# Shared expert of a mixture-of-experts step: three products of high and low parts instead of one float32 product, and a ring of four for its sums

## What is computed

```python
def swiglu(x, wg, wu, wd):
    return (jax.nn.silu(x @ wg) * (x @ wu)) @ wd

routed = routed_experts(hf, eidx, gw, w_e_gate, w_e_up, w_e_down, blk)
shared = swiglu(hf, w_s_gate, w_s_up, w_s_down)
return (routed + shared).astype(h.dtype).reshape(B, S, D)
```

## Time and profile before

| | us |
|---|---|
| median of 3 runs (2080.31 to 2085.21) | 2081.19 |
| the profiled execution | 2073.48 |
| its span, first to last instruction | 2071.7 |
| PE busy | 1910.6 |
| DVE busy | 1318.2 |
| ACT busy | 996.6 |

### The profile page before, as it was taken

How to read it: one execution, slowest core, us unless ns; L and a number is a source line. 1 busy time by engine, 2 the same in 40 slices (tenths; PEclk the granted TensorE clock), 3 DMA queues, 4 the chain that set the end, 5 groups by cost and what they waited for, 6 DMA issues and landing times. The chain is left out here.

```text
span 2071.7 us, 38132 instructions
## 1 busy us (share of the span) xinstructions
PE 1910.6 (92%) x13128; PEld 1493.1 (72%) x13128; DVE 1318.2 (64%) x1974; ACT 996.6 (48%) x1537; POOL 759.1 (37%) x672
## 2 busy tenths in 40 slices
PE   7999899969799999999898989998999999999994
PEld 5787778857455689888687637777777777777773
DVE  4389767775789831111557636776777777777772
ACT  6322123356576621111334116766777766776762
POOL 2111123343445211100026713455436645445642
PEclk9999999989899999999999999999999999999997
DMA  7488831066577859870633258999999999999995
GB/s 238 139 287 268 275 121 42 19 189 182 188 225 230 265 194 291 270 249 21 216 107 103 85 212 297 352 350 319 350 356 356 349 341 354 348 353 343 345 324 141
DMA packets 170943, 501.87 MB, mean 242 GB/s; under 512 B 26326, under 2 KB 71956, under 8 KB 144396
## 3 DMA queue, kind: packets, MB, share of 16 engines
q1 hardware_dynamic: 128164, 353.65, 47.2%
q0 software_dynamic: 31680, 80.82, 15.5%
q10 hardware_dynamic: 10992, 66.02, 9.5%
HBM read 437.87 MB, written 120.75 MB: 270 GB/s over the span
## 5 line engine op out<-in xcount | busy, mean ns | idle before, releaser
L2769 DVE TENSOR_TENSOR w_gu_lo<-turned,w_gu_hi 128x2048 fp32r<-128x2048 f32 x132 | 302.8, 2294 | 103.9 <-ACT w_gu_hi L2683 103.9
L2683 ACT ACTIVATE w_gu_hi<-turned 128x2048 fp32r<-128x2048 f32 x132 | 252.5, 1914 | 39.9 <-PEq L1931 39.9
L2531 POOL DMA_INDIRECT x_scratch<-turned,target x66 | 133.1, 2017 | 318.3 <-DMA x_scratch<-turned,target 262.8
L668 PE MATMUL pP<-wring,hT_hi 128*128 128x512 f32 (+2 forms) x520 | 206.3, 397 | 17.3 <-DVE wring L594 6.5
L2606 PE MATMUL pG_e<-w_gu_hi,xT_hi 128*128 128x512 f32 x528 | 216.8, 411 | 0.0
L2606 PE MATMUL pG_e<-w_gu_lo,xT_hi 128*128 128x512 f32 x528 | 209.9, 397 | 0.0
L2606 PE MATMUL pG_e<-w_gu_hi,xT_lo 128*128 128x512 f32 x528 | 209.4, 397 | 0.0
L670 PE MATMUL pP<-wring,hT_lo 128*128 128x512 f32 (+2 forms) x520 | 201.2, 387 | 0.0
L669 PE MATMUL pP<-wring,hT_hi 128*128 128x512 f32 (+2 forms) x520 | 201.1, 387 | 0.0
L2792 DVE TENSOR_TENSOR w_e_lo<-turned,w_e_hi 128x2048 fp32r<-128x2048 f32 x66 | 151.0, 2288 | 20.8 <-ACT w_e_hi L2697 20.8
L412 POOL TENSOR_TENSOR wring<-turned,wring 128x512 fp32r<-128x512 f32 (+1 forms) x43 | 70.8, 1675 | 222.2 <-ACT wring L448 221.9
(11 more groups left out here) (354 smaller groups left out, 4582.9 us busy)
## 6 DMA issues: line engine op xcount, KB each, us to landing
turned<-in_w_e_up SPq DMA_DIRECT2D x65, 1024.0 KB, 9.4
turned<-in_w_e_down SPq DMA_DIRECT2D x65, 1024.0 KB, 11.3
turned<-in_cache_sb_kv SPq DMA_DIRECT2D x256, 256.0 KB, 3.2
turned<-in_w_e_gate SPq DMA_DIRECT2D x64, 1024.0 KB, 6.9
out<-in_cache_win_kv ACTq DMA_DIRECT2D x8, 4094.0 KB
turned<-in_w_in ACTq DMA_DIRECT2D x56, 256.0 KB, 6.3
turned<-in_w_in SPq DMA_DIRECT2D x16, 512.0 KB, 7.8
out<-in_cache_win_kv ACTq DMA_DIRECT2D x8, 1022.0 KB
```

The source lines that it names most:

```text
L668: pe.matmul(pP[:m, b, :w], hi, w_hi(u), start=(c == 0), stop=False)
L2531: pool.indirect_dma_start(sc["x2"], bass.IndirectOffsetOnAxis(ap=target[:, j, 0:1], axis=0), y[j], None, bounds_check=T - 1, oob_is_err=Fa ...
L2683: act.activation(ghi[:, r, k, :, :].rearrange("p c f -> p (c f)"), w[:, r, k, :], ACT.Copy).then_inc(ghi_ready, 1)
L2769: dve.tensor_tensor(glo[:, r, k, :, :].rearrange("p c f -> p (c f)"), w[:, r, k, :], ghi[:, r, k, :, :].rearrange("p c f -> p (c f)").bitc ...
```

## The change

The shared expert's products are made of parts. ACT copies the two halves of `ws_gu`, each third of `h2T`, `wd` and each unit of the hidden values to fp32r (`high_weight`, `high_third`, the copy to `wd_hi`, `high_hidden`), DVE subtracts (`low_weight`, `low_third`, `low_down`, `low_hidden`). The parts lie in `w_o_hi`, `w_o_lo`, `mix_hi` and `mix_lo`, which the projection no longer needs by then. So a unit of gate and up has 48 matmuls and a tile of the last product 12. The low and high part of a third share one buffer over all three thirds (`third_read`), and `wd_lo` lies where `wgu_lo` lay.

With `w_o_hi` in use, x1 is reloaded into the ring of the sums, now four deep (`XRING`): four tiles at once, and each further one when the store four tiles back has landed. The first unit stands ahead of the sixth tile's places on PE and starts a tile of x1 earlier. On DVE the sixth tile's choice is made behind the first splits. Four of the nine tiles of the last product (`EARLY_DOWN`) stand ahead of the table's transposes on PE, and their sums ahead of the table on DVE. `count_blocks` is cut in two, and the second half (`place_blocks`) follows two more hidden instructions.

```diff
-    last_x1 = late[:NS, :D]
-    x2 = late[:, 2 * D:4 * D].rearrange("p (n d) -> p n d", d=D)
+    x2 = late[:, :XRING * D].rearrange("p (n d) -> p n d", d=D)
...
+        wgu_hi, wgu_lo = (wo_lo_flat[:, q * NWGU:(q + 1) * NWGU].rearrange("p (k c f) -> p k c f", k=2, c=KC) for q in range(2))
+        third_hi, third_lo = (chunks(wo_hi_flat[:, q * NTHIRD:(q + 1) * NTHIRD]) for q in range(2))
...
-                for t in range(NT):
-                    sp.dma_start(x1_row(t), sc["x1"][t * P:t * P + rows_of(t), :]).then_inc(xs_in, 16)
+                def reload(t):
+                    if t >= XRING:
+                        sp.wait_ge(x2_out[t % XRING], 16 * (t // XRING))
+                    sp.dma_start(x2[:rows_of(t), t % XRING, :], sc["x1"][t * P:t * P + rows_of(t), :]).then_inc(xs_in[t % XRING], 16)
+                for t in range(XRING):
+                    reload(t)
                 for t in range(NT):
...
                     sp.wait_ge(x2_ready, t + 1)
-                    sp.dma_start(sc["x2"][t * P:t * P + m, :], x2[:m, t % 2, :]).then_inc(x2_out[t % 2], 16)
-                for i in range(2):
-                    sp.wait_ge(x2_out[i], 16 * len(range(i, NT, 2)))
+                    sp.dma_start(sc["x2"][t * P:t * P + m, :], x2[:m, t % XRING, :]).then_inc(x2_out[t % XRING], 16)
+                    if t >= 1 and t + XRING - 1 < NT:
...
                 def gate_up(i):
...
-                    if i == 0:
-                        pe.wait_ge(ws_in, 48)
                     if i < 2:
-                        pe.wait_ge(x1_ready, NT)
+                        pe.wait_ge(x1_ready, NP + i)
                     else:
                         pe.wait_ge(silu_ready, i - 1)
-                    for k in range(2):
-                        for c in range(KC):
-                            last = pe.matmul(pG[:, i % 2, k, :NC], wgu[:, k, c, f * P:(f + 1) * P], h2T[:, c, n * NC:(n + 1) * NC],
-                                             start=(c == 0), stop=(c == KC - 1))
+                    for product in range(3):
+                        if product == 0:
+                            pe.wait_ge(wgu_hi_ready, 2)
+                            pe.wait_ge(third_hi_ready, n + 1)
+                        if product == 1:
+                            pe.wait_ge(wgu_lo_ready, 2)
+                        if product == 2:
+                            pe.wait_ge(third_lo_ready, n + 1)
+                        wt = wgu_lo if product == 1 else wgu_hi
+                        rows = third_lo if product == 2 else third_hi
+                        for k in range(2):
+                            for c in range(KC):
+                                last = pe.matmul(pG[:, (i + 1) % 2, k, :NC], wt[:, k, c, f * P:(f + 1) * P], rows[:, c, :],
+                                                 start=(product == 0 and c == 0), stop=(product == 2 and c == KC - 1))
+                        if product == 1:
+                            last.then_inc(third_read, 1)
                     last.then_inc(gu_ready, 1)
+                def down(t):
...
+                    if t >= 2:
+                        pe.wait_ge(x2_ready, t - 1)
+                    else:
+                        pe.wait_ge(silu_ready, NGU - 1 + t)
+                    pe.wait_ge(wd_hi_ready, 1)
+                    pe.wait_ge(hid_lo_ready, NF * ((t * P + m - 1) // NC + 1))
+                    for product in range(3):
+                        if product == 2:
+                            pe.wait_ge(wd_lo_ready, 1)
+                        for k in range(2):
+                            wt = wd_lo if product == 2 else wd_hi
+                            for f in range(NF):
+                                low = lo_main[:, f, t * P:t * P + m] if t < NP else lo_tail[:, f, :]
+                                rows = low if product == 1 else hid_hi[:, f, t * P:t * P + m]
+                                last = pe.matmul(pY[:m, (t + 1) % 2, k * 512:(k + 1) * 512], rows, wt[:, f, k * 512:(k + 1) * 512],
+                                                 start=(product == 0 and f == 0), stop=(product == 2 and f == NF - 1))
+                    last.then_inc(shared_ready, 1)
                 for b in range(NT + 3):
                     if b == 0:
@@ -2099,31 +2164,25 @@
                         turn(b - 1)
                     if 0 <= b - 2 < NT:
                         router(b - 2)
+                    if b in (NP, NP + 1):
+                        gate_up(b - NP)
                     if 0 <= b - 3 < NT:
                         place(b - 3)
-                    if b >= NP:
+                    if b > NP + 1:
                         gate_up(b - NP)
-                for i in range(4, NGU - 1):
+                for i in range(4, NGU):
                     gate_up(i)
                 pe.wait_ge(eb_ready, 1)
                 pe.matmul(pR[0:1, :NBLK], eb[:NBLK, 1:2], ident[:NBLK, :NBLK], start=True, stop=True).then_inc(eb_psum, 1)
-                gate_up(NGU - 1)
+                for t in range(EARLY_DOWN):
+                    down(t)
                 pe.wait_ge(tablef_ready, 1)
...
                 pe.transpose(pT[:, 3 * P:3 * P + NBLK], tail_weight, ident[:NBLK, :NBLK]).then_inc(table_psum, 1)
-                pe.wait_ge(silu_ready, NGU)
-                pe.wait_ge(hid_ready, NGU)
-                for t in range(NT):
...
-                    if t >= 2:
-                        pe.wait_ge(x2_ready, t - 1)
-                    for k in range(2):
-                        for f in range(NF):
-                            last = pe.matmul(pY[:m, t % 2, k * 512:(k + 1) * 512], hid[:, f, t * P:t * P + m], wd[:, f, k * 512:(k + 1) * 512],
-                                             start=(f == 0), stop=(f == NF - 1))
-                    last.then_inc(shared_ready, 1)
+                for t in range(EARLY_DOWN, NT):
+                    down(t)
...
+                def high_weight(k):
...
+                    act.wait_ge(ws_in, 48)
+                    act.activation(wgu_hi[:, k, :, :], wgu[:, k, :, :], ACT.Copy).then_inc(wgu_hi_ready, 1)
+                def high_third(n):
...
+                    act.wait_ge(h2T_ready, third_last[n] + 1)
+                    if n >= 1:
+                        act.wait_ge(third_read, NF * n)
+                    act.activation(third_hi, h2T[:, :, n * NC:(n + 1) * NC], ACT.Copy).then_inc(third_hi_ready, 1)
+                def high_hidden(i):
...
+                    act.wait_ge(hid_ready, i + 1)
+                    act.activation(hid_hi[:, f, n * NC:(n + 1) * NC], hid[:, f, n * NC:(n + 1) * NC], ACT.Copy).then_inc(hid_hi_ready, 1)
...
+                    if b == NT - 1:
+                        high_weight(0)
...
+                    if b == NT - 1:
+                        high_third(0)
+                        high_weight(1)
...
+                    if b == NT:
+                        high_third(1)
...
+                act.activation(wd_hi, wd, ACT.Copy).then_inc(wd_hi_ready, 1)
                 for i in range(2, NGU):
+                    if i == 2 * NF - 1:
+                        high_third(2)
                     gate(i)
+                    high_hidden(i - 2)
+                high_hidden(NGU - 2)
+                high_hidden(NGU - 1)
...
+                def low_weight(k):
+                    dve.wait_ge(wgu_hi_ready, k + 1)
+                    dve.tensor_tensor(wgu_lo[:, k, :, :], wgu[:, k, :, :], wgu_hi[:, k, :, :].bitcast(F32), ALU.subtract).then_inc(wgu_lo_ready, 1)
+                def low_third(n):
+                    dve.wait_ge(y_ready, NT)
+                    dve.wait_ge(third_hi_ready, n + 1)
+                    if n >= 1:
+                        dve.wait_ge(gu_ready, NF * n)
+                    dve.tensor_tensor(third_lo, h2T[:, :, n * NC:(n + 1) * NC], third_hi.bitcast(F32), ALU.subtract).then_inc(third_lo_ready, 1)
+                def low_down():
+                    dve.wait_ge(wd_hi_ready, 1)
+                    dve.wait_ge(third_read, NGU)
+                    dve.tensor_tensor(wd_lo, wd, wd_hi.bitcast(F32), ALU.subtract).then_inc(wd_lo_ready, 1)
...
+                def add_shared(t):
...
+                    dve.wait_ge(shared_ready, t + 1)
+                    dve.wait_ge(xs_in[t % XRING], 16 * (t // XRING + 1))
+                    dve.tensor_tensor(x2[:m, t % XRING, :], pY[:m, (t + 1) % 2, :], x2[:m, t % XRING, :], ALU.add).then_inc(x2_ready, 1)
...
-                    if 0 <= b - 3 < NT:
+                    if 0 <= b - 3 < NT and b != NT - 1:
                         choose(b - 3)
                     if 0 <= b - 4 < NT:
                         list_pairs(b - 4)
+                    if b == NT + 1:
+                        low_third(1)
                     if b in (NT + 1, NT + 2):
                         hidden(b - NT - 1)
+                    if b == NT - 1:
+                        low_weight(0)
                     if b < NT:
...
                         dve.wait_ge(y_ready, b + 1)
@@ -2345,32 +2476,41 @@
...
```

(34 more changed lines are left out.)

61 lines of the change are left out of this document (54 added, 7 removed).

## The result

The changed kernel takes 2090.26 us (median of 20 runs, 2079.76 to 2099.8), the kernel before 2081.3 (20 runs, 2070.35 to 2090.32): ratio 1.0036, 95% interval 1.0021 to 1.0051. It is slower by 0.36%: little, but the interval excludes no change. 2077.6 was predicted, with a range of 2072 to 2085.5.

A forecast was written before the change was run, and what follows sets the result against it. PE was taken to bound the stage; of 17.4 us saved there, the ring's landings let 3.6 us through (next phase 1232.4 for 1236.0), so 2081.19 - 3.6 = 2077.6 us, range 2072 to 2085.5.

The forecast's parts named there:

- What PE saves: Shared expert's products on PE: 10.6 us less over six units, 6.8 us less over nine tiles, 17.4 us in all.
- The start: First gate and up unit on PE: starts at 1134.8, 4.1 us late, and ends at 1144.6.
- The middle is DVE's: Seventh tile's places to first sum: DVE's work sets the pace, last places at 1168.4, PE idle some 3 us, first sum ends 1201.0.
- The charge of 1.8 us for that gap: Fourth unit on PE, behind the idle time before the last places: low clock costs 1.8 us.
- The step that failed: Fourth unit: second product ends at 1176.1, then ACT overwrites the third, copy to 1178.6.
- The ring: Last product's sums: chained stores and reloads end the last sum at 1228.0, next phase at 1232.4 for 1236.0.
- The fast rival: Last product: store 0 and reload 4 land in some 5 us each, PE's gain arrives, 7.7 us faster, 2073.5; chance 0.27.
- The ring as slow rival: Last product: reload 4 and store 4 also take 10.3 us each, 6.6 us slower, 2087.8; chance 0.13.
- The small one: POOL: DVE's long subtractions hold up its scatters, and the table comes later than its 5.6 us of slack; chance 0.05.

The follow-up runs named there:

- few_after: The changed kernel with one scatter of eight sent for the last four tiles, 28 left out: 2061.78 us, 0.9864 to 0.9933 of the kernel before.
- few_after2: few_after repeated in more rounds, the changed kernel with 28 scatters left out: 2064.81 us, 0.9890 to 0.9948 of the kernel before.
- before_b: The kernel before, unchanged, profiled a second time: 2107.43 us in one run.
- float_last: The changed kernel with its last two gate and up units float32 on the third itself, third copy and its subtraction left out: 2095.00 us.

## Why the prediction was wrong, step by step

- **What PE saves.** Right. Units of 7.83 us for 7.7, tiles of 2.8 for 2.73 (four tiles from 1218.50 on, their sums 2.79 apart).
- **The start.** Right: the first unit at 1134.54 for 1134.8, its end at 1143.8 for 1144.6.
- **The middle is DVE's.** Right up to the last places, 1167.87 for 1168.4, with 2.35 us of PE idle for "some 3", and a granted clock of 0.64 and 0.51 behind it (1168 to 1172). The charge of 1.8 us for that gap does not always fall due: few_after was idle for 2.31 us there and its fourth unit took 9.35 us at a clock down to 0.50, few_after2 was idle for 2.30 and its unit took 7.83 at 1.00.
- **The step that failed** is the next one, "its second product ends at 1176.1, and only then may ACT overwrite the third: copy to 1178.6". The product ended at 1175.6. The copy ended at 1200.06. The step took a signal of PE to arrive when its matmul ends, as all did in the profile of before; beside a train of POOL's scatters it came 21.9 us late. few_after has the copy from 1176.25 to 1178.75, so up to here the sum was right but for this step.
- **Why only the changed kernel pays in full.** The kernel before has the same scatters, and held signals in before_b, but there PE runs up to two units of 9.5 us ahead of ACT's gates before it needs one. In the changed kernel PE's next unit needs ACT's copy at once. Leaving the scatters out took 18 us off one (2083.7 to 2066.0) and some 27 off the other (2091 to 2064): the 9 between are the result. In the profiles it moved the next phase by 0 to 11.7 us in the kernel before and by 21.6 to 26.1 in the changed one, so part of both gains lies behind the stage. And the sum was made on an execution without the hold-up, 2073.48, of a kernel with a median of 2081; what the median holds beyond it was carried over as a constant, as if the change could not touch it.
- **What hides behind it.** In few_after2, without the hold-up, PE ended the units and waited 0.37 us for low_down, as foretold. These are its sums on DVE, the first and the last five of nine:

```profile
1199.59 1.22 DVE L2421 TENSOR_TENSOR turned<-pY,turned 128x1024 f32<-128x1024 f32 x1
...
1217.82 1.22 DVE L2421 TENSOR_TENSOR turned<-pY,turned 128x1024 f32<-128x1024 f32 x1 [4.33 <-DMA turned<-x_scratch]
1222.27 1.23 DVE L2421 TENSOR_TENSOR turned<-pY,turned 128x1024 f32<-128x1024 f32 x1 [3.22 <-DMA turned<-x_scratch]
1226.50 1.22 DVE L2421 TENSOR_TENSOR turned<-pY,turned 128x1024 f32<-128x1024 f32 x1 [3.01 <-DMA turned<-x_scratch]
1229.85 1.23 DVE L2421 TENSOR_TENSOR turned<-pY,turned 128x1024 f32<-128x1024 f32 x1 [2.12 <-DMA turned<-x_scratch]
1231.42 1.21 DVE L2421 TENSOR_TENSOR turned<-pY,turned 8x1024 f32<-8x1024 f32 x1 [0.34 <-DMA turned<-x_scratch]
```

- **The ring.** Right in kind and nearly in size: the first sum ends at 1200.8 for 1201.0, store 0 lands 10.7 us after its issue for 10.3, and the fifth sum starts at 1217.8 for 1217.3; from the fifth on each waits for a reload. Undersized was what follows: of the five late reloads I let only the first and the last count, for the fifth and the ninth sum, but the sixth, seventh and eighth sum stood 4.5, 4.2 and 3.4 us behind the one before, each at its reload, so that the ninth started at 1231.4, not 1226.7, and the next phase at 1234.9 for 1232.4. Of the foretold 3.6 us nothing is left in the profiles on average (1235.8 and 1234.9 in the changed kernel, 1234.8 and 1236.1 in the one before, all without the 28 scatters), and 1.7 in the means, with an interval that holds both. Even without the hold-up, then, the saving of 3.6 us is not shown.
- **The fast rival** is excluded with the hold-up or without it: no profile has the next phase below 1234.7. Its rule, that queues take turns packet by packet (the Trainium skill, DMA: Bandwidth & Descriptors, Queues, rings and completion order), gave 5.1 us for a store; in few_after2 the stores' median landing is 7.5 us and the five reloads took 3.6 to 7.1, in the changed kernel 8.0 and 2.9 to 8.5. These runs show the landings, not the order of the packets.
- **The ring as slow rival** did not happen. The small one, subtractions against POOL's scatters, is there in kind: one scatter of 3.50 us beside `low_third`, 2.5 us longer. The train's end, and with it the release, comes that much later.

## What to carry to other kernels

Before a change puts a round trip between engines on the critical path, look at what else runs at that time, in more than one profile: the latency of a signal is measured only for the traffic beside which it was measured. A wait that the profile puts down to "remote", together with "issue" gaps of PE, while POOL sends indirect transfers back to back, was the sign of this hold-up here. Fewer scatters beside the round trip took it away. Slack of two units between PE's signal and its need lessened it (10.4 us at the next phase in before_b, 21.6 and more in the changed kernel), and a single removed wait moved the loss on (float_last). Where executions of one kernel spread over 1%, ask which of them was profiled before adding up against it.
